# A wait ahead of GpSimd's product of the shared expert's down weights with the gate rows

## The reference

```python
def moe_ffn(xf, w_router, b_router, we_gate, we_up, we_down, ws_gate, ws_up, ws_down):
    top_idx, top_w = route(xf, w_router, b_router)
    routed = routed_experts(xf, top_idx, top_w, we_gate, we_up, we_down)
    shared = (jax.nn.silu(xf @ ws_gate) * (xf @ ws_up)) @ ws_down
    return routed + shared
...
        h_lat = h_lat + gt_fl * y[:b * n].reshape(b, n, d)
        h_ctx = h_ctx + gt_fc * y[b * n:].reshape(b, n_ctx, d)
```

## Time and profile before

| | us |
|---|---|
| median of 3 runs | 2620.27 (2620.18 to 2622.15) |
| the profiled execution's own time | 2621.41 |
| its span (first to last instruction) | 2619.6 |
| PE busy | 2352.7 (90%) |
| DVE busy | 831.7 (32%) |
| ACT busy | 654.7 (25%) |
| POOL busy | 278.7 (11%) |

### The profile page before, as it was taken

The page is one execution under the profiler, slowest core; times in us unless marked ns, Lnnn a source line. Parts: engine busy times, 40 slices in busy tenths (PEclk is TensorE's granted clock), DMA queues, the critical chain, the costliest instruction groups (busy, mean ns, idle before and its releaser), DMA issues. The chain is left out here.

```text
span 2619.6 us, 34138 instructions
## 1 busy us (share of the span) xinstructions
PE 2352.7 (90%) x13484; PEld 1243.6 (47%) x13484; DVE 831.7 (32%) x1715; ACT 654.7 (25%) x1413; POOL 278.7 (11%) x260
## 2 busy tenths in 40 slices
PE   6999999799899999999993879998889998989874
PEld 3544555475544333333331768886644333333322
DVE  2332556526511010100104945555462000000005
ACT  1111444421011212121212444444311111111111
POOL 1000000031011111111110000000211111111100
PEclk9999999999999999999997989999999999989997
DMA  8566200112479999999985611100347999999967
GB/s 330 194 225 210 97 1 1 69 65 109 187 295 358 375 378 405 390 369 379 382 317 210 260 37 37 37 25 1 141 181 309 415 419 419 420 418 407 411 277 312
DMA packets 122205, 646.55 MB, mean 247 GB/s; under 512 B 18648, under 2 KB 29912, under 8 KB 60352
## 3 DMA queue, kind: packets, MB, share of 16 engines
q1 hardware_dynamic: 92512, 556.21, 54.4%
q0 software_dynamic: 29248, 87.12, 8.5%
q10 hardware_dynamic: 288, 1.05, 0.1%
HBM read 604.38 MB, written 57.75 MB: 253 GB/s over the span
## 5 line engine op out<-in xcount | busy, mean ns | idle before, releaser
L1564 PE MATMUL E_psG<-E_gu,E_xT 128*32 128x512 f32 (+2 forms) x2544 | 531.8, 613 | 44.7 <-DMA E_gu<-in_we_up_dram 29.1
L1858 DVE TENSOR_TENSOR E_hh<-E_sil,E_psG 128x256 f32<-128x256 f32 x96 | 40.4, 421 | 1082.6 <-ACT E_sil L1697 1082.6
L1564 PEld LDWEIGHTS E_psG<-E_gu,E_xT 128*32 128x32 f32 (+2 forms) x2544 | 157.0, 122 | 288.8 <-issue 281.8
L1578 PE MATMUL E_psY<-E_dn,E_hT 128*32 128x512 f32 (+2 forms) x1272 | 261.9, 596 | 1.5 <-ACT E_hT L1700 1.5
L1564 PE MATMUL E_psG<-fT,E_xT 128*32 128x512 f32 (+2 forms) x704 | 239.2, 623 | 3.5 <-DMA E_gu<-in_we_up_dram 3.1
L1564 PE MATMUL E_psG<-o,E_xT 128*32 128x512 f32 (+2 forms) x736 | 225.3, 611 | 6.0 <-DMA E_gu<-in_we_up_dram 6.0
L1697 ACT ACTIVATE E_sil<-E_psG 128x256 f32<-128x256 f32 x96 | 36.9, 384 | 658.3 <-PE E_psG L1564 658.3
L1439 POOL DMA_INDIRECT y_d<-E_yb,E_sca x94 | 94.3, 1004 | 984.4 <-ACT E_yb L1703 984.4
L1703 ACT ACTIVATE E_yb<-E_psY,E_wgt 128x1024 f32<-128x1024 f32 x96 | 107.0, 1115 | 289.4 <-PE E_psY L1578 289.4
L1564 PE MATMUL E_psG<-raw,E_xT 128*32 128x512 f32 (+2 forms) x464 | 148.3, 594 | 1.2 <-DVE E_xT L1855 1.2
L1557 PEld LDWEIGHTS E_psX<-cst,E_tmp 128*128 128x128 f32 x768 | 94.2, 193 | 73.3 <-issue 73.3
(11 more groups left out here) (396 smaller groups left out, 3724.0 us busy)
## 6 DMA issues: line engine op xcount, KB each, us to landing
E_gu<-in_we_gate_dram SPq DMA_DIRECT2D x70, 1024.0 KB, 11.2
E_gu<-in_we_up_dram SPq DMA_DIRECT2D x70, 1024.0 KB, 15.9
E_dn<-in_we_down_dram SPq DMA_DIRECT2D x70, 1024.0 KB, 15.0
h<-in_w_ada_dram SPq DMA_DIRECT2D x40, 1024.0 KB, 4.8
o<-in_we_gate_dram SPq DMA_DIRECT2D x24, 1024.0 KB, 12.1
o<-in_we_up_dram SPq DMA_DIRECT2D x24, 1024.0 KB, 15.6
o<-in_we_down_dram SPq DMA_DIRECT2D x24, 1024.0 KB, 15.1
I_ring<-y_d SPq DMA_DIRECT2D x24, 1024.0 KB, 7.1
```

Of the source, the lines that this page charges most:

```text
L1564: ins = nc.tensor.matmul(psG[c:c + n, 0].rearrange("p (v f) -> p v f", v=2), xT[:, k, c:c + n], slots[s][0][:, :, k], start=(k == 0), stop ...
L1578: ins = nc.tensor.matmul(psY[c:c + w, n], hT[:, j, k, c:c + w], slots[s][1][:, k, n * 512:(n + 1) * 512], start=(k == 0), stop=(k == KF - 1))
L1858: V.tensor_tensor(hh[:], sil[:], psG[:, 0, FF:2 * FF], ALU.mult).then_inc(done, 1)
```

## The change

GpSimd waits for `s_free` before it starts the products. The hidden product of the first block (`hidden(0)`, L1430) stays ahead of the wait, the others stay behind the products.

```diff
                         hidden(0)
                         pool.wait_ge(s_gt, 16 * nv)
                         pool.wait_ge(s_wd_, 16)
+                        pool.wait_ge(s_free, 1)
                         if nv > 1:
                             G.tensor_tensor(wds[1], wd, bc(yb[:, 1], KF), ALU.mult).then_inc(s_fold, 1)
                             pool.wait_ge(s_fold, 1)
                         G.tensor_tensor(wd, wd, bc(yb[:, 0], KF), ALU.mult).then_inc(s_fold, 1)
                         for t in range(1, nt):
                             hidden(t)
```

## The result

The changed kernel takes 2624.37 us (median of 16 runs, 2619.41 to 2633.78), the kernel before on the same chip 2620.22 us (2610.29 to 2625.31). The ratio is 1.0033, 95% interval 1.0021 to 1.0044: 8.6 us slower (5.5 to 11.5). Weighted together they are 8.3 us, 6.1 to 10.4. The forecast was 4.7 us slower.

What follows compares the result with a forecast made beforehand. TensorE's passage through each opening was taken as the bound, set by VectorE's chain in layer 0. Layer 0's loss of 6.5 less layer 1's gain of 1.8 made 4.7 us slower, 2625.0 us; range 2622.5 to 2628.

Steps and rivals of the forecast that it cites:

- Products hold VectorE: Both openings: a GpSimd product holds VectorE operations with two SBUF inputs until it ends; MAX8, with one input, passes.
- The rival of no holds: Both layers: GpSimd's products don't hold VectorE; sum 4.1 to 2.1 us faster, 2616 to 2618; chance 0.06.
- the 0.15 us that a held operation saves: VectorE: a held operation ends about 0.28 us after its holder, against an estimated 0.43 alone, saving 0.15 us.
- Layer 0's gain, 1.8 us: Layer 0's opening: L1795 no longer held, so L1514 moves from 642.00 to 640.2, gaining 1.8 us in VectorE's chain.
- The hold of L1812, 4.2 us: Layer 0's opening: the first product holds VectorE's L1812 until 649.1 instead of 644.9, a loss of 4.2 us.
- The race between VectorE and GpSimd for the release: Layer 0: one semaphore releases L1811 and the first product; L1811 assumed to win, otherwise the sum is the same within 0.3.
- The hold of L1817, 3.3 us, and two L1430 at 0.4: Layer 0's opening: the second product delays L1817 by 3.3 us; two L1430 behind it cost VectorE 0.4 us each, 0.8 together.
- The clock (the rival didn't come): Layer 0: half clock lasting into the second table and down product costs 1.5 us more, 2626.5 up to 2628; chance 0.12.
- Layer 1's gain, 1.8 us, passed on one for one: Layer 1's opening: TensorE 2.7 us earlier, keeps 2.0 after waiting for the second table, put at 1.8, reaching the end whole.
- the second half of the step: Layer 1's loop: the weight stream starts as early as TensorE does, so the opening's gain or loss passes one for one.
- The rival of a swallowed gain: Layer 1's loop: the full weight stream doesn't start sooner, so the gain is lost; 2626.8 us; chance 0.11.

Runs made afterwards that it cites:

- e10_before_again: The kernel before, unchanged, run again as a measure of scatter; ratio 0.9999 (0.9986 to 1.0012).
- e4_noprod: The kernel before without GpSimd's products of down weights with gate rows; 2655.65 us, a total not comparable because layer 1's tokens took other experts.
- e6_hahead: The changed kernel with layer 0's hidden product of block 1 (L1430) ahead of the wait; 2621.35 us, run once, not timed against the kernel before.
- e3_second: The changed kernel, but in layer 0 the first product runs at once and only the second waits; 2618.94 us, ratio 0.9993 to the kernel before.
- e5_fill: The changed kernel with 12 useless matmuls in TensorE's idle time before layer 0's first table; 2625.58 against 2617.52 us for the kernel before, ratio 1.0026.
- e1_l0only: The changed kernel with the wait for s_free kept in layer 0 alone; 2625.04 against 2619.66 us for the kernel before, ratio 1.0028.
- e9_delay1: The kernel before with 24 idle matmuls on TensorE ahead of layer 1's tables; 2632.54 against 2620.38 us, ratio 1.0050.
- e7_late: The kernel before with one layer 0 product at once, the other after two block additions, layer 1's after its second table; 2615.17 against 2617.52 us.
- e8_latefill: e7_late plus idle matmuls before layer 0's first table and between layer 1's small products; 2611.85 us, ratio 0.9981 to the kernel before.

## Why the prediction came out as it did

**Products hold VectorE (right, the reason drawn too narrow).** L1813 and L1818, with two inputs in SBUF, were held wherever a product lay beside them, and MAX8 never. But "operations with two inputs in SBUF" isn't the whole list: L1795, L1781 (in `e10_before_again`) and the changed kernel's L1827 are TENSOR_SCALAR with one tensor in SBUF, and were held too (2.76, 4.50 and 0.75 us), while VectorE's operations that read PSUM weren't (L1793 and L1794 of before ran beside the second product and took 0.33 and 0.23 us). It changed nothing in the sum. The rival of no holds (faster) is out: it needed holds of less than 4.5 us, they were 8.5. The Trainium skill, "SBUF — State Buffer", section "SBUF: two separate sides", gives as mechanism an exclusive lock on a shared pair of ports, between a GpSimd instruction and a VectorE operation that has two SBUF inputs or runs in a two-port mode; the trace agrees (L1813, 4.74 us), but for the 0.15 us that a held operation saves, which it doesn't mention.

**Layer 0's gain, 1.8 us (right).** Measured from the first L1528, L1515 is at 11.92 us instead of 13.72, and `e4_noprod` starts its table 1.80 us earlier. I had written that the L1430 of blocks 1 and 2 ran apart from operations that can be held. Block 1's didn't: it ran from 640.25 to 640.97, and L1796 beside it took 0.65 us instead of 0.20. VectorE so gains 3.0 us up to L1800 and not 2.57, but TensorE is in L1528 until then and the sum is the same.

**The hold of L1812, 4.2 us (right).** 4.74 less 0.56 is 4.18. The race between VectorE and GpSimd for the release went as assumed: VectorE's first operation behind the release (L1812 in the changed kernel's numbers, as in the next sentence) started 0.14 us before the product. The products' rows are 4.78 and 4.69 us long, but each stood first behind an operation of VectorE: from the ends of L1812 (638.13) and L1813 (642.90) they took 4.36 and 4.35, predicted 4.37.

**The hold of L1817, 3.3 us, and two L1430 at 0.4 (the second a little small).** 8.05 less 3.70 is 4.35, of which two L1430 at 0.54 (`e6_hahead`) are 1.08 and the product 3.27. The sum for layer 0 is 4.18 + 4.35 - 1.80 = 6.73 us; the table starts 6.78 us later in the profiled executions, and 6.7 in the mean of all with the wait against those without it (`e10_before_again` left out; with it, 5.8). Predicted: 6.5. The loop then passes it on whole, 723.5 us in every trace.

**The clock (the rival didn't come).** Half clock is there after both idle pieces, but not longer than before: the table pair takes 9.07, 8.12 and 9.19 us with the wait, and 8.04, 8.95, 9.19, 9.53 and 8.03 us in unchanged code of layer 0.

**Layer 1's gain, 1.8 us, passed on one for one (this step failed).** Its first part was right: L1515 comes 2.70 us earlier counted from the opening's start, and the product costs VectorE 1.5 us. The size failed. I had put 0.8 for the L1430: two that collide newly, at 0.4 each. Two did, but cost 0.53 and 0.57 us, and the third, which had already cost 0.41 (L1841), cost 0.53: 1.2 in all. The second table comes at 36.64 us from the opening's start instead of 33.92, 2.7 later and not 2.3, and TensorE waits 1.48 us for it and not 0.7. The opening is then 39.4 us in five of the seven traces with the wait, and 39.7 and 39.9 in `e3_second` and `e5_fill`, where L1528 took 23.38 and 23.17 us. That is 1.3 less than in before's first trace at the best, but only 0.4 to 0.5 less than in `e10_before_again` and `e1_l0only`, and 0.6 in the mean. In the trace that I predicted from, L1528 took 23.16 us at a granted clock of 0.90, against 22.22 and 22.31 at 0.94 and 0.93, so some of the apparent gain is the clock's.

Then there is the second half of the step, "So there too the stream of weights starts as early as TensorE does". `e9_delay1` bears it out for a delay. For a gain D+E shows 0.2 us in the mean, but within a scatter that leaves it undecided. With what the traces show in place of my 1.8 us, the sum is between 6.1 (0.6 us of gain) and 6.5 (0.2 us), inside the measured 6.1 to 10.4; my 4.7 is outside. The rival of a swallowed gain, to which I gave 0.11, came out nearer (6.5 us slower), but that the stream swallows a gain isn't shown: that there was less to gain than 1.8 us is.

**What stays open.** The middle of the measured interval, 8.3 us, is 1.5 to 2 us above what the openings explain. The other parts of the program give no place for it: counted from the last down product of layer 0 to layer 1's first L1495, the traces with the wait in layer 0 have 525.9 to 530.8 us and those without it 528.3 to 530.7; before layer 0's opening and behind layer 1's loop they overlap in the same way. The separate timings of the layers (7.3 slower, uncertain by 3.4, and 2.8 faster, by 2.1) don't settle it: they sum to 4.5, uncertain by 4. Nor do they agree with the traces on layer 1, where 0.6 to 4.9 us faster would leave room for my 1.8. Whether a gain ahead of layer 1's loop arrives is open: loops of the same code differ by 3.6 us (583.52 to 587.15).

**What the comparison could tell.** I set 0.2% as the bound of what can be told and the forecast just inside it. The loss was 0.3%, and two comparisons tell it from no change.

## What to carry to other kernels

Before a long GpSimd operation is moved, list what VectorE does in the stretch where it will land: here each operation with two SBUF inputs, and TENSOR_SCALAR from SBUF, stood still until it ended, however short it was. What counts is how much of the product is still to run when the chain reaches such an operation: a 0.2 us operation met a product with 2.7 us still to run and lost 2.6 us, 1.8 of them on the way to the tables, and another met one at its start and lost 4.3 us. The two products beside the chain's long run cost 4.2 and 3.3 us. Put them where VectorE is idle, as `e7_late` does, or has MAX8 or PSUM work. And ahead of a loop bound by DMA, don't take a gain for certain because a delay is paid: a delay of 10 us arrived whole in the one trace that has it, while an opening shorter by 0.6 us in the mean can't be told from none in loops that scatter by 3.6 us.

## What the hardware did that I hadn't expected

The executions of the kernel before on one chip lie up to 15 us apart (2610.29 to 2625.31), and the traces show one place: code that the change doesn't touch. The granted clock in the output stage of layer 0 (50 us, columns as in rows 1), first in the changed kernel, then in its second trace:

```profile
570.00:620.00 50.00, 45.39 (x223) 33.50 (x221) 27.53 (x110) 12.89 (x19) 8.78 (x4) 1.00 0.27 94
```

```profile
570.00:620.00 50.00, 46.66 (x194) 33.93 (x194) 25.90 (x103) 15.13 (x23) 8.06 (x3) 0.90 0.21 74
```

With 1.00 the first L1528 starts at 622.09 us, with 0.90 at 629.35; before has 0.91 and 628.28, `e8_latefill` 1.00 and 623.42. That is 5 to 7 us, as much as the change, and it is why each trace here was read from a mark inside the stage.

GpSimd, waiting behind a VectorE operation, gets in between two operations that don't wait for each other: the two L1430 got in among the six L1818 and cost 0.54 us each, less than their 0.73 us alone.
